# More seven-product pairs in five gate parts, and their last additions moved from VectorE to ScalarE copies and adding DMA

## The chip, the cores and the metric

The kernel runs on one core of a Trainium2 chip, in float32. The metric is the device time of one execution in microseconds. TensorE's clock is granted at its upper level of 2.4 GHz throughout (mean 0.998 of it in the profiled execution).

## The reference, cut to what matters

One layer of a streaming encoder for 256 positions and 2048 channels. The normalised input is projected at once into everything that three attention branches need, and into three gates; the gate projections and the branch projections are where the change lies:

```python
h = _rmsnorm(x, ln_g[l])                                  # 256 x 2048
(qa, ..., zc, ga, gb, gc) = _split_cols(h @ w_in[l])      # ga, gb, gc: 2048 columns each
ya = _mixer_a(...) * jax.nn.silu(za)                      # three attention branches, 256 x 1024 each
yb = _mixer_b(...) * jax.nn.silu(zb)
yc = _mixer_c(...) * jax.nn.silu(zc)
merged = (jax.nn.sigmoid(ga) * (ya @ w_pa[l])
          + jax.nn.sigmoid(gb) * (yb @ w_pb[l])
          + jax.nn.sigmoid(gc) * (yc @ w_pc[l]))
x = x + merged @ w_o[l]
return _rmsnorm(x, final_g)
```

## The kernel before, in words

**Products.** Every float32 matrix product is made of three matmuls of rounded operands: high x high, high x low, low x high. The high part of a weight piece (`w_hi`) is a rounded copy made by ScalarE (L612), the low part (`w_lo`) is the difference made by VectorE (L854). The weights come from HBM in pieces of 128 x 1024 (512 KB) into the slots of `raw`, six of them (`RAWS`); w_hi and w_lo live in a ring of six pieces (`RING`), so ScalarE may write the w_hi of piece n only when TensorE is through with piece n-6. In the stage that matters here both engines prepare a piece four pieces ahead (`FAR`). SyncE loads the slots in order of the pieces, each as soon as VectorE is through with what lay in it: for the first two pieces of a seven-product pair that is after the pair's second sum (waits at L511 and L513).

**Chunks.** The work is a fixed list of chunks, each cut into pieces; each engine runs through the same list with a program of its own. After the attention stage come three branches (b = 0, 1, 2), each as G, P, P, G, P, P. A G chunk ("gate part") computes 1024 columns of one gate projection over all 2048 rows of the weight; a P chunk computes 512 columns of the branch projection, four pieces of four products each. Then come the output chunks, one of which is made like a gate part. The gate part G(b, 0) is called (b, 0) below, the other one (b, 1).

**Pairs.** A gate part's 2048 rows are 16 blocks of 128, taken as eight pairs. For a plain pair ("hh" in the order string of `group_pieces`) TensorE makes eight block products of 128 x 128 x 512, from two pieces of four products. For a seven-product pair ("S") it makes seven, as in the method of Strassen and Winograd: a full piece with two products ("11 22"), a half piece with one ("21 12"), and two pieces of two products that aren't loaded but are sums of the first two, made by VectorE in `usum` ("U1 U3", "U2 U4"). The sums are `sum_13` (L1046, called the first sum here) and `sum_24` (L1056, L1058, the second sum); VectorE issues them at six and five pieces ahead of the piece "U1 U3". All gate parts but the first, (0, 0), have five seven-product pairs and three plain ones, 59 products; (0, 0) has four and four.

**End of a gate part.** The products lie in all eight banks of PSUM. Before the last piece ScalarE copies two banks (`copy_sums`, L718 and L719), VectorE makes four additions with two further banks (`combine`, L1098 to L1105, called the combine), and when TensorE is through, two large additions of the last four banks (`finish_sums`, L1113, called the finish). ScalarE then takes the tanh (L725) at the first two pieces of the following P chunk. A P chunk's result is multiplied by the gate by VectorE (`merge_chunk`, the merge), at the end of the first P chunk and at the first piece of the gate part after the second. For some P chunks of b = 1 and 2 the addition into `merged` is made by an adding DMA that GpSimd issues (L596); the finish writes into the same tile `gx` that holds the gates.

**Who waits.** TensorE waits at the start of a chunk (`banks_free`) until the banks are read out: for a gate part, until the first P chunk before it is merged; for the P chunk behind a gate part, until `copy_sums` is done; for the next one, until the finish is done.

Of the kernel before, what the change touches and what calls it, by code (L numbers as in the profile page):

```python
# [10 lines left out]
ACT = mybir.ActivationFunctionType  # L11

P = 128
# [17 lines left out]

NS = 5
NS_OUT = 3
# [7 lines left out]
def group_pieces(b, u):  # L41

    order = "hhShhShhShhhh" if b == 3 else FIRST_ORDER if (b, u) == (0, 0) else "hShShShShSh"
    n = order.count("S")
    pieces, summed, plain = [], 0, 0
    for k in order:
        if k == "S":
            pieces += [(part, summed) for part in ("11 22", "21 12", "U1 U3", "U2 U4")]
            summed += 1
        else:  # L50
            pieces.append((("p 11 22", "p 21 12")[plain % 2], n + plain // 2))
            plain += 1
    return pieces
# [32 lines left out]
RAW_OF = {g: d for d, g in enumerate(LOADED)}  # L86
ADDED_BY_DMA = [(1, 0), (1, 1), (1, 2), (1, 3), (2, 0), (2, 1)]
COPIED = ("kvc", "v", "uv")
SUMMED = ("q", "k", "uk", "ka")
# [7 lines left out]
RING = 6  # L97
RAWS = 6
WARM = 8
# [99 lines left out]
def hybrid_trunk(nc, x, x_t, w_s, bias, ckv_g, sink, final_g, out):  # L199
# [3 lines left out]
    with ExitStack() as ctx:  # L203
# [45 lines left out]
        with ExitStack() as attention:  # L249
            def early_sb(name, shape):  # L250
                return attention.enter_context(nc.sbuf_tensor(name, shape, F32))

            k_b = early_sb("k_b", [P, 8, SEQ])
            v_b = early_sb("v_b", [P, NT, BW])
            kT_a = early_sb("kT_a", [P, 2, SEQ])
            v_a = early_sb("v_a", [P, NT, 2 * HD])
            v_mid = early_sb("v_mid", [P, 2 * HD])
            work = early_sb("work", [P, SROW])
            causal = early_sb("causal", [P, SROW])
            chosen = early_sb("chosen", [P, SROW])  # L260
            scores = early_sb("scores", [P, 4, SROW])
            probsT = early_sb("probsT", [P, 4, SROW])
            bias_t = early_sb("bias_t", [P, 2, 2, SROW])
            silu = early_sb("silu", [P, 2, SEQ])
# [79 lines left out]
        p_mul = sem("p_mul")  # L344
        merged_added = sem("merged_added")

        zeroed = sem("zeroed")
# [85 lines left out]
        def half_of_sums(k, again):  # L433

            return slice(2, NS_OUT if again else NS) if k else slice(0, 2)

# [123 lines left out]
        def _(pool):  # L560
# [23 lines left out]
            for p in range(NPAIR):  # L584
                if 8 <= p < 16:
# [5 lines left out]
                    pool.wait_ge(bm_ready, 32 * (p - 7))  # L591
            for k, (b, n) in enumerate(ADDED_BY_DMA):
                c = AT["P", b, n]
                pool.wait_ge(dve_evac, dves_before(c + 1))
                wait(pool, merged_added, 16 * k)
                pool.dma_start(merged_v[:, :, CH * n:CH * (n + 1)], gate_of(c), accum_op=ALU.add  # L596
                               ).then_inc(merged_added, 16)
            for t in range(NT):
# [6 lines left out]
        def _(sc):  # L605
# [106 lines left out]
            def copy_sums(c):  # L712
# [6 lines left out]
                nc.scalar.copy(sums[1], bank[3][:, :]).then_inc(g_copied, 1)  # L719

            def tanh_sums(c, parts):

                for a in parts:
                    sc.wait_ge(g_final, NT * sums_of(c) + a // 2 + 1)
                    nc.scalar.activation(gx[:, a, :], gx[:, a, :], ACT.Tanh, scale=0.5).then_inc(tanh_ready, 1)  # L725
# [20 lines left out]
            for c, (kind, b, u) in enumerate(CHUNKS):  # L746
                for j in range(PIECES[c]):
# [50 lines left out]
                    if kind == "G" and j == LAST_SUM[c] + 1:  # L798
                        copy_sums(c)
                    if kind == "P" and KINDS[c - 1] == "G" and j < 2:  # L800
                        tanh_sums(c - 1, (2 * j, 2 * j + 1))
                    if (kind, b, u) == ("P", 2, 3) and j >= 1:
                        transpose_hi(2 * j - 2)
# [11 lines left out]
                    if c == LAST_O and j in (3, 6):  # L815
                        t = j // 6
                        sc.wait_ge(sum_ready, 2 * t + 4)
                        nc.scalar.activation(merged_v[:, t, middle], out_rows[t][:, middle], ACT.Square,
                                              accum_out=ssq_o[:, t, 1:2]).then_inc(sq_ready, 1)
                if kind in ("v", "uv"):  # L820
                    copy_chunk(c)
# [25 lines left out]
        def _(ve):  # L847
# [189 lines left out]
            def sum_13(g):  # L1037
# [3 lines left out]
                wait_source(ve, g - 1)  # L1041
                if SUMS.index(g) == 0:
                    ve.wait_ge(pT_ready, 2 * NPAIR)
                elif SUMS.index(g) == 1:
                    ve.wait_ge(pv_ready, NPAIR // 2)
# [127 lines left out]
            for c, (kind, b, u) in enumerate(CHUNKS):  # L1173
                for j in range(PIECES[c]):
# [108 lines left out]
                    if g in YT_AT:  # L1283
                        yT_split(*YT_AT[g])
                    if kind == "G" and j == 0 and KINDS[c - 1] == "P":
                        merge_chunk(c - 1)
                    if kind == "G" and j == LAST_SUM[c] + 1:
                        combine(c, 0)
                    if kind == "G" and j == min(LAST_SUM[c] + 2, PIECES[c] - 1):
                        combine(c, 1)  # L1290
                    if g + FAR + 2 in SUMS:
                        sum_13(g + FAR + 2)
                    if g + FAR + 1 in SUMS:
                        sum_24(g + FAR + 1)
                    if g == GATES + 1:
# [23 lines left out]
                if kind == "z":  # L1319
                    silu_chunk(c)  # L1320
                if kind == "G" and b < 3:
                    finish_sums(c)
                if kind == "P" and KINDS[c + 1] != "G":
                    merge_chunk(c)
# [39 lines left out]
        def _(pe):  # L1364
# [9 lines left out]
            def banks_free(c):  # L1374
# [17 lines left out]
                if kind == "G":  # L1392
                    pe.wait_ge(g_final, NT * sums_of(c))

# [386 lines left out]
```

## Time and profile before

| | |
|---|---|
| three runs | 943.28, 943.40 and 943.66 us, median 943.4 |
| profiled execution | 943.88 us, its span 941.8 |
| busy: TensorE | 932.6 us, 99% |
| busy: VectorE | 761.8 us, 81% |
| busy: ScalarE | 536.1 us, 57% |
| DMA, mean | 209 GB/s |

A row of time shows the start, the length, the engine, the line and the tiles (out<-in); idle time before it and what ended it stand in brackets. Matmuls are pipelined: each row is longer than the step from one start to the next, so steps are read from the starts. The same holds for VectorE and ScalarE, whose rows overlap the next one by about 0.1 us.

### The profile page before, as it was taken

Reading aid. Unit: us, or ns where it says so; the run is one execution under the profiler, and the core shown is the slowest. Engines: PE = TensorE matmul, PEld = TensorE weight load, DVE = VectorE, ACT = ScalarE, POOL = GpSimd, SP = SyncE. Lnnn points to the kernel's source line nnn. Section 1 sums busy time; section 2 is a strip of 40 time slices with the busy share of each in tenths; the row PEclk is TensorE's granted clock in tenths of the full one; section 3 lists DMA queues with packets and bytes.
Section 4 is the critical chain, followed back from the end, with each engine's and each line's share of the span. In section 5 each row is a group of like instructions: output and inputs, shape, how many; then the busy total and the mean of one; then the engine's idle time right before and its main releaser. Section 6 shows DMA issues by size and latency. Waiting matters only on the chain.

```text
span 941.8 us, 13769 instructions
## 1 busy us (share of the span) xinstructions
PE 932.6 (99%) x5066; PEld 793.2 (84%) x5066; DVE 761.8 (81%) x1306; ACT 536.1 (57%) x916; POOL 32.5 (3%) x40
## 2 busy tenths in 40 slices
PE   9999999999999999999999999999999999999996
PEld 8888888888888888888888888888888888888885
DVE  6585765777756777889998899899997988988993
ACT  6573544466535565667755556465564664654552
POOL 0020000000011110000000000000001000000000
PEclk9999999999999999999999999999999999999999
DMA  8964743666567775556556557467667597664552
GB/s 329 339 206 140 250 157 124 214 231 230 181 183 224 224 224 191 190 191 212 180 180 244 179 187 247 164 208 231 216 223 224 201 373 207 244 224 135 179 179 89
DMA packets 58706, 196.67 MB, mean 209 GB/s; under 512 B 6544, under 2 KB 9488, under 8 KB 58000
## 3 DMA queue, kind: packets, MB, share of 16 engines
q1 hardware_dynamic: 54128, 188.71, 57.9%
q0 software_dynamic: 3936, 6.29, 3.8%
q8 instruction: 40, 0.66, 0.3%
q10 hardware_dynamic: 576, 0.79, 0.2%
q14 instruction: 26, 0.21, 0.1%
HBM read 187.38 MB, written 2.10 MB: 201 GB/s over the span
## 4 chain that ended last, share of the span: by engine, by line
PE 94%; DMA 2%; DVE 1%; issue 1%; SPq 0%; ACT 0%; POOLq 0%; POOL 0%; DVEq 0%
PE bank L1431 24%; PE bank L1441 13%; PE bank L1482 10%; PE bank L1483 10%; PE bank L1481 10%; PE bank L1406 7%; PE bank L1407 7%; PE bank L1408 7%; DMA raw<-in_w_s_dram 2%; PE bank L1368 2%; PE bank L1542 1%; PE bank L1572 1%; DVE w_lo L854 1%; PE bank L1565 0%; PE bank L1690 0%
## 5 line engine op out<-in xcount | busy, mean ns | idle before, releaser
L854 DVE TENSOR_TENSOR w_lo<-raw,w_hi 128x1024 fp32r<-128x1024 f32 (+2 forms) x328 | 369.2, 1154 | 48.0 <-ACT w_hi L612 46.9
L612 ACT ACTIVATE w_hi<-raw 128x1024 fp32r<-128x1024 f32 (+2 forms) x328 | 318.6, 1003 | 71.5 <-PE bank L1408 29.3
L1431 PE MATMUL bank<-hT,w_hi 128*128 128x512 f32 x976 | 236.4, 392 | 0.0
L1431 PEld LDWEIGHTS bank<-hT,w_hi 128*128 128x128 f32 x976 | 178.4, 188 | 34.4
L1441 PE MATMUL bank<-hT,w_lo 128*128 128x256 f32 x976 | 132.1, 284 | 0.0
L1441 PEld LDWEIGHTS bank<-hT,w_lo 128*128 128x128 f32 x976 | 126.4, 191 | 6.6 <-issue 0.9
L612 ACT ACTIVATE w_hi<-usum 128x1024 fp32r<-128x1024 f32 x64 | 68.1, 1064 | 94.9 <-DVE usum L1046 55.9
L1481 PE MATMUL bank<-w_hi,hT 128*128 128x512 f32 x288 | 112.0, 389 | 0.0
L1482 PE MATMUL bank<-w_lo,hT 128*128 128x512 f32 x288 | 112.0, 389 | 0.0
L1483 PE MATMUL bank<-w_hi,hT 128*128 128x512 f32 x288 | 112.0, 389 | 0.0
L854 DVE TENSOR_TENSOR w_lo<-usum,w_hi 128x1024 fp32r<-128x1024 f32 x64 | 78.1, 1222 | 6.7 <-ACT w_hi L612 6.6
L1406 PE MATMUL bank<-w_hi,ybuf 128*128 128x512 f32 x200 | 78.3, 391 | 0.1
L665 ACT ACTIVATE gate<-bank 128x256 f32<-128x256 f32 x69 | 22.7, 383 | 97.0 <-PE bank L1431 88.6
L1407 PE MATMUL bank<-w_lo,ybuf 128*128 128x512 f32 x200 | 77.8, 389 | 0.0
L1481 PEld LDWEIGHTS bank<-w_hi,hT 128*128 128x128 f32 x288 | 54.1, 188 | 11.3
L1482 PEld LDWEIGHTS bank<-w_lo,hT 128*128 128x128 f32 x288 | 54.1, 188 | 11.2
L1483 PEld LDWEIGHTS bank<-w_hi,hT 128*128 128x128 f32 x288 | 54.1, 188 | 11.2
L1408 PE MATMUL bank<-w_hi,ybuf 128*128 128x512 f32 x136 | 52.9, 389 | 0.0
L1408 PE MATMUL bank<-w_hi,hT 128*128 128x512 f32 x128 | 49.8, 389 | 0.0
L1481 PE MATMUL bank<-w_hi,s_hi 128*128 128x512 f32 x128 | 49.8, 389 | 0.0
L1482 PE MATMUL bank<-w_lo,s_hi 128*128 128x512 f32 x128 | 49.8, 389 | 0.0
L1483 PE MATMUL bank<-w_hi,s_lo 128*128 128x512 f32 x128 | 49.8, 389 | 0.0
(212 smaller groups left out, 1116.6 us busy)
## 6 DMA issues: line engine op xcount, KB each, us to landing
raw<-in_w_s_dram SPq DMA_DIRECT2D x314, 512.0 KB, 4.5
bias_t<-in_bias_dram SPq DMA_DIRECT2D x24, 384.0 KB, 3.2
bias_t<-chosen POOLq DMA_DIRECT2D x16, 192.0 KB, 6.8
merged<-big POOLq DMA_DIRECT2D x6, 512.0 KB, 7.2
raw<-in_w_s_dram SPq DMA_DIRECT2D x6, 456.0 KB, 7.6
merged<-in_x_dram SPq DMA_DIRECT2D x2, 1024.0 KB, 14.5
raw<-in_w_s_dram SPq DMA_DIRECT2D x8, 256.0 KB, 3.3
big<-in_x_dram SPq DMA_DIRECT2D x1, 2048.0 KB, 10.1
```

Of the source, the lines that this page charges most:

```text
L612: nc.scalar.activation(halves(g)[0], source(g), ACT.Copy).then_inc(hi_ready, 1)
L665: nc.scalar.activation(gate[:, n % 2, SEQ:CH] if KINDS[c] != "iq" else gate[:, n // 2, SEQ * (n % 2):SEQ * (n % 2 + 1)], bank[base(c) + n] ...
L854: nc.vector.tensor_tensor(low, source(g), high.bitcast(F32), ALU.subtract).then_inc(lo_ready, 1)
L1368: return nc.tensor.transpose(dst, src, ident[0:n, 0:n])
L1406: mm(acc, xh, wh[:, e, :], start=kt == 0, stop=False)
L1407: mm(acc, xh, wl[:, e, :], start=False, stop=False)
L1408: ins = mm(acc, xl, wh[:, e, :], start=False, stop=kt == n_kt - 1)
L1431: ins = mm(bank[base(c) + n][:, :], wh[:, e, n * P:(n + 1) * P], hl_t[:, n_kt * j + e, :, :], start=j == 0 and e == 0, stop=last and e == ...
L1441: ins = mm(bank[base(c) + n][:, 0:SEQ], wl[:, e, n * P:(n + 1) * P], hl_t[:, n_kt * j + e, 0, :], start=False, stop=last and e == n_kt - 1)
L1481: mm(acc, left[0], wh, start=start, stop=False)
L1482: mm(acc, left[0], wl, start=False, stop=False)
L1483: return mm(acc, left[1], wh, start=False, stop=stop)
```

## The change

Five gate parts, all but (0, 0), have six seven-product pairs and two plain ones, 58 products, in the order h SS h SS h SS h. To find room for the larger sums of h, `raw` has five slots instead of six. The finish of every gate part but the last, (2, 1), is made in another way: ScalarE copies the last four banks into the half of `usum` that is free (`copy_rest`), and GpSimd issues two DMAs of 512 KB each that add them to `gx`. The tanh moves to the second and third piece of the second P chunk, the merge of the first P chunk to the fourth piece of the second. The second seven-product pair of each changed part has its sums issued three pieces sooner. The first sum of all waits for the last attention product (`pv_ready`) instead of the last transposes (`pT_ready`).

```diff
-NS = 5
+NS = 6
 NS_OUT = 3
...
-    order = "hhShhShhShhhh" if b == 3 else FIRST_ORDER if (b, u) == (0, 0) else "hShShShShSh"
+    order = "hhShhShhShhhh" if b == 3 else FIRST_ORDER if (b, u) == (0, 0) else "hSShSShSSh"
     n = order.count("S")
...
 ADDED_BY_DMA = [(1, 0), (1, 1), (1, 2), (1, 3), (2, 0), (2, 1)]
+LAST_GROUP = AT["G", 2, 1]
+LAST_U = {c: max(g for g in SUMS if PART[g][0] == c) for c in USES}
+SOON = [3 if PART[g][0] != AT["G", 0, 0] and sum(PART[k][0] == PART[g][0] for k in SUMS[:n]) == 1 else 0
+        for n, g in enumerate(SUMS)]
 COPIED = ("kvc", "v", "uv")
...
 RING = 6
-RAWS = 6
+RAWS = 5
 WARM = 8
...
         merged_added = sem("merged_added")
+        rest_copied = sem("rest_copied")
+        rest_added = sem("rest_added")
...
-            return slice(2, NS_OUT if again else NS) if k else slice(0, 2)
+            m = NS_OUT if again else NS
+            return slice((m + 1) // 2, m) if k else slice(0, (m + 1) // 2)
+
+        def finish_parts(c):
+
+            return usum[:, SUMS.index(LAST_U[c]) % 2, :, :]
...
                     pool.wait_ge(bm_ready, 32 * (p - 7))
-            for k, (b, n) in enumerate(ADDED_BY_DMA):
-                c = AT["P", b, n]
-                pool.wait_ge(dve_evac, dves_before(c + 1))
-                wait(pool, merged_added, 16 * k)
-                pool.dma_start(merged_v[:, :, CH * n:CH * (n + 1)], gate_of(c), accum_op=ALU.add
-                               ).then_inc(merged_added, 16)
+            for c, (kind, b, n) in enumerate(CHUNKS):
+                if kind == "G" and c < LAST_GROUP:
+                    pool.wait_ge(g_comb, 4 * sums_of(c) + 4)
+                    for t in range(NT):
+                        pool.wait_ge(rest_copied, NT * sums_of(c) + t + 1)
+                        pool.dma_start(gx[:, 2 * t:2 * t + 2, :].rearrange("p n s -> p (n s)"),
+                                       finish_parts(c)[:, t, :], accum_op=ALU.add).then_inc(rest_added, 16)
+                if kind == "P" and (b, n) in ADDED_BY_DMA:
+                    pool.wait_ge(dve_evac, dves_before(c + 1))
+                    wait(pool, merged_added, 16 * ADDED_BY_DMA.index((b, n)))
+                    pool.dma_start(merged_v[:, :, CH * n:CH * (n + 1)], gate_of(c), accum_op=ALU.add
+                                   ).then_inc(merged_added, 16)
             for t in range(NT):
...
+            def copy_rest(c):
+
+                sc.wait_ge(used, FIRST[c + 1])
+                for t in range(NT):
+                    nc.scalar.activation(finish_parts(c)[:, t, :].rearrange("p (n s) -> p n s", n=2),
+                                         pair[2 + t][:, :, :], ACT.Copy).then_inc(rest_copied, 1)
+
             def tanh_sums(c, parts):
+                if c < LAST_GROUP:
+                    sc.wait_ge(rest_added, 32 * sums_of(c) + 32)
                 for a in parts:
-                    sc.wait_ge(g_final, NT * sums_of(c) + a // 2 + 1)
+                    if c == LAST_GROUP:
+                        sc.wait_ge(g_final, a // 2 + 1)
                     nc.scalar.activation(gx[:, a, :], gx[:, a, :], ACT.Tanh, scale=0.5).then_inc(tanh_ready, 1)
...
                         copy_sums(c)
-                    if kind == "P" and KINDS[c - 1] == "G" and j < 2:
+                    if kind == "P" and c - 1 == LAST_GROUP and j < 2:
                         tanh_sums(c - 1, (2 * j, 2 * j + 1))
+                    if kind == "P" and KINDS[c - 2] == "G" and c - 2 < LAST_GROUP and j in (1, 2):
+                        tanh_sums(c - 2, (j - 1, j + 1))
                     if (kind, b, u) == ("P", 2, 3) and j >= 1:
...
                                               accum_out=ssq_o[:, t, 1:2]).then_inc(sq_ready, 1)
+                if kind == "G" and c < LAST_GROUP:
+                    copy_rest(c)
                 if kind in ("v", "uv"):
...
                 wait_source(ve, g - 1)
-                if SUMS.index(g) == 0:
-                    ve.wait_ge(pT_ready, 2 * NPAIR)
-                elif SUMS.index(g) == 1:
+                if SUMS.index(g) < 2:
                     ve.wait_ge(pv_ready, NPAIR // 2)
...
                         yT_split(*YT_AT[g])
+                    if kind == "P" and KINDS[c - 2] == "G" and c - 2 < LAST_GROUP and j == 3:
+                        merge_chunk(c - 1)
                     if kind == "G" and j == 0 and KINDS[c - 1] == "P":
...
                         combine(c, 1)
-                    if g + FAR + 2 in SUMS:
-                        sum_13(g + FAR + 2)
-                    if g + FAR + 1 in SUMS:
-                        sum_24(g + FAR + 1)
+                    for n, k in enumerate(SUMS):
+                        if k - FAR - 2 - SOON[n] == g:
+                            sum_13(k)
+                        if k - FAR - 1 - SOON[n] == g:
+                            sum_24(k)
                     if g == GATES + 1:
...
                     silu_chunk(c)
-                if kind == "G" and b < 3:
+                if c == LAST_GROUP:
                     finish_sums(c)
-                if kind == "P" and KINDS[c + 1] != "G":
+                if kind == "P" and KINDS[c + 1] != "G" and c > LAST_GROUP:
                     merge_chunk(c)
...
                 if kind == "G":
-                    pe.wait_ge(g_final, NT * sums_of(c))
+                    pe.wait_ge(g_comb, 4 * sums_of(c))
+                    if c - 2 == LAST_GROUP:
+                        pe.wait_ge(g_final, NT)
+                    else:
+                        pe.wait_ge(rest_copied, NT * sums_of(c))
```

## Rows read from the trace of the kernel before

**Rows 1.** Page, the chain that ended last: share of the span by engine.

```profile
PE 94%; DMA 2%; DVE 1%; issue 1%; SPq 0%; ACT 0%; POOLq 0%; POOL 0%; DVEq 0%
```

**Rows 2.** Waits of TensorE, all of them: total us, times, longest us.

```profile
PE bank L1596 <- DVE hT L1159: 1.4, 1, 1.4
```

**Rows 3.** Busy time by stages: one period (G, P, P), us busy of each engine.

```profile
578.00:640.00 62.00, 62.00 (x275) 51.33 (x274) 56.26 (x58) 35.78 (x40) 0.00 (x0) 1.00 0.60 204
```

**Rows 4.** Timeline of TensorE: first matmul of gate part (1, 0), and first behind it.

```profile
597.85 0.39 PE L1481 MATMUL bank<-w_hi,hT 128*128 128x512 f32 x1
...
637.97 0.39 PE L1406 MATMUL bank<-w_hi,y_odd_hi 128*128 128x512 f32 x1
```

**Rows 5.** Timeline of VectorE around and in gate part (1, 0).

```profile
593.76 1.23 DVE L854 TENSOR_TENSOR w_lo<-usum,w_hi 128x1024 fp32r<-128x1024 f32 x1
...
598.05 1.22 DVE L1028 SCALAR_TENSOR_TENSOR merged<-big,bank 128x1024 f32<-128x1024 f32 x1 [0.34 <-PE bank L1408]
...
601.92 1.23 DVE L854 TENSOR_TENSOR w_lo<-raw,w_hi 128x1024 fp32r<-128x1024 f32 x1 [1.50 <-ACT w_hi L612]
603.06 1.22 DVE L1046 TENSOR_TENSOR usum<-raw 128x1024 f32<-128x1024 f32 x1
604.20 0.68 DVE L854 TENSOR_TENSOR w_lo<-raw,w_hi 128x512 fp32r<-128x512 f32 x1
604.80 0.69 DVE L1056 TENSOR_TENSOR usum<-usum,raw 128x512 f32<-128x512 f32 x1
605.52 0.69 DVE L1058 TENSOR_TENSOR usum<-usum,raw 128x512 f32<-128x512 f32 x1
606.13 2.44 DVE L854 TENSOR_TENSOR w_lo<-usum,w_hi 128x1024 fp32r<-128x1024 f32 x2
608.49 2.35 DVE L854 TENSOR_TENSOR w_lo<-raw,w_hi 128x1024 fp32r<-128x1024 f32 x2
...
631.57 5.76 DVE L854 TENSOR_TENSOR w_lo<-raw,w_hi 128x1024 fp32r<-128x1024 f32 x5
637.24 0.68 DVE L1098 TENSOR_TENSOR big<-big,bank 128x512 f32<-128x512 f32 x1
...
640.07 2.35 DVE L1113 TENSOR_TENSOR big<-big,bank 128x1024 f32<-128x1024 f32 x2
```

**Rows 6.** Timeline of ScalarE in the same part: a w_hi, and the two bank copies.

```profile
600.83 1.06 ACT L612 ACTIVATE w_hi<-raw 128x1024 fp32r<-128x1024 f32 x1 [1.66 <-PE bank L1483]
...
635.45 0.59 ACT L718 COPY big<-bank 128x512 f32<-128x512 f32 x1 [0.23 <-PE bank L1483]
635.93 0.59 ACT L719 COPY big<-bank 128x512 f32<-128x512 f32 x1
```

**Rows 7.** DMA: loads (L514, 670 to 690), adding DMAs (L596), their queue (651 to 660).

```profile
DMA to landing us min/median/max: 3.4/3.5/4.6
...
DMA to landing us min/median/max: 6.9/7.2/8.8
...
q0 software_dynamic: 272, 0.52, 31.9%
```

**Rows 8.** Around the end of part (2, 0): issue of x, a stage (last but one: DMA share), a w_hi.

```profile
753.98 0.42 SPq L545 DMA_DIRECT2D big<-in_x_dram  x1
...
768.00:772.00 4.00, 4.00 (x20) 3.30 (x19) 2.27 (x2) 4.00 (x6) 0.00 (x0) 1.00 1.03 414
...
772.97 1.06 ACT L612 ACTIVATE w_hi<-raw 128x1024 fp32r<-128x1024 f32 x1 [0.15 <-DMA raw<-in_w_s_dram]
```

**Rows 9.** Startup: a load in the chain (issue to landing), and TensorE's wait behind it.

```profile
18.86 15.31 DMA raw<-in_w_s_dram
...
36.57 0.19 PEld L1406 LDWEIGHTS bank<-w_hi,ybuf 128*128 128x128 f32 x1 [0.55 <-DVE w_lo L854]
```

**Rows 10.** Last attention products on TensorE, and VectorE's first sum of all.

```profile
469.06 1.53 PE L1542 MATMUL bank<-probsT,rows 128*64 128x128 f32 x24
...
468.20 1.22 DVE L1046 TENSOR_TENSOR usum<-raw 128x1024 f32<-128x1024 f32 x1
```

More of the change, by code:

```diff
@@ L260, in hybrid_trunk @@
             chosen = early_sb("chosen", [P, SROW])
+            early_sb("s_end", [P, P])
             scores = early_sb("scores", [P, 4, SROW])
```

## The prediction

> **What bounds the kernel now.** The chain of waits comes first: 94% of the span is TensorE [rows 1]. The waits of TensorE name one, 1.4 us at the start [rows 2]; in the gate stage it never waits. The view by stages shows how near the next engine is: of 62 us (one period: a gate part and two P chunks) VectorE is busy 56.3, ScalarE 35.8 [rows 3]. So TensorE is the bound, VectorE 5.7 us behind it, and where those 5.7 us lie decides this case. TensorE's timeline gives the unit: gate part (1,0) starts at 597.85 and the P chunk behind it at 637.97, 59 products of three matmuls in 40.12 us, 0.680 us per product u [rows 4]; a P chunk of 16 products is 10.9 us. VectorE's timeline [rows 5] shows an idle 1.50 us before 601.92 and then one unbroken run from 603.06 to 637.2, through the whole gate part. Its steps, start to start (us): w_lo of a full piece 1.14 (601.92 to 603.06; two usum pieces from 606.13 to 608.49, 1.18 each), of a half piece 0.60; the first sum of a pair 1.14, the second 0.72 + 0.61 = 1.33; a merge 1.15; a finish 2.27 for both halves. A seven-product pair costs it 1.14 + 1.14 + 0.60 + 1.33 + 2.36 = 6.56, while TensorE spends 7u = 4.76 on it. A plain pair, two pieces, costs 2.27 against 8u = 5.44 on TensorE. Seven-product pairs are lost ground for VectorE and plain pieces win it back: 7.69 against 11u = 7.48 for one pair and one plain piece.
>
> **What TensorE saves.** Five gate parts have 58 products instead of 59: 5 x 0.680 = 3.4 us. If nothing else moved: 940.0.
>
> **Load of VectorE.** Per changed part +6.56 - 2.27 for the pair and -2.27 for the finish: +2.0 in a period of 61.5, so 58.3 busy. On the average it still fits. It must be followed in order, since the ring of six pieces forbids it to run ahead: w_hi of piece n waits until TensorE has begun piece n-5, 0.26 later (piece 6 of the part shown at 600.83, TensorE's piece 1 at 597.85 + 4u), and w_lo follows 1.09 behind, at 601.92 [rows 5, 6].
>
> Time 0 is TensorE's start of the gate part. Its order is h SS h SS h SS h (pieces 0 to 27); a pair takes 2u, 1u, 2u, 2u, an h 4u. TensorE begins piece 1 at 4u = 2.7, 2 at 6u = 4.1, 16 at 32u = 21.8, 21 at 43u = 29.3, 25 at 50u = 34.0, and ends at 58u = 39.5. VectorE's w_lo of piece 3 starts at -4.1 as before (593.76), then come the merge of the first P chunk to -1.8, the second sum of pair 2 to -0.4 (issued three pieces sooner than the rule for the others has it, its first sum is done by then), w_lo of 4 to 0.7, the merge of the second P chunk to 1.9, w_lo of 5 to 3.0; piece 6 waits for the ring to 3.6, piece 7 to 5.4 (4.08 + 0.26 + 1.09). From there it is unbroken: pieces 7 and 8 2.36; 9 and 10 2.27; rest of pair 3 (both sums, the half piece, two usum pieces) 5.43; piece 14 1.14; rest of pair 4 5.43; 18 and 19 2.27; rest of pair 5 5.43; 23 1.14; first sum, piece 24 and second sum of pair 6 1.14 + 0.60 + 1.33. That is 28.5: piece 25 starts at 33.95 and is written 1.22 later, at 35.2. TensorE wants it at 34.0. Margins at 16 and 21 are 0.9 and 0.7; at 25 it is -1.2. By the same count the order of before has at least 2 us everywhere (its w_lo of piece 25 is through at 632.7, wanted at 635.3). I take **1.17 us per part, 5.8 us** in all; bounds 0.5 and 1.9 per part (a semaphore step more or less at each of some five hand-overs of ScalarE).
>
> **End of the gate part.** Copies and combine stand behind the w_hi and w_lo of the fourth piece of the next chunk. With five raw slots the third and fourth wait for the slots of pair 6, free with its second sum at 33.95. A load lands 3.5 us later [rows 7], the second 1.3 behind: 38.8; w_hi to 39.8; two bank copies of 0.48 + 0.59 [rows 6] to 40.8, and TensorE, which waits for them before the P chunk, is there at 39.5 + 1.2 = 40.6. Before, the same copies began at 635.45, 2.5 early. I take **0.2 per part, 1.0**; from 0 to 1.0 each (loads land up to 4.6 after issue).
>
> **The finish by ScalarE and DMA.** Let E be TensorE's end of the part. The two bank copies (some 1.0 each, twice the 0.48 of a half) are done by E+2.3. VectorE, late now, ends w_lo at E+1.4 and the combine (2.83, 637.24 to 640.07) at E+4.2, and POOL issues only then: E+4.25 and, after 1.2, E+5.45. An adding DMA of this size exists in the trace: 6.9 to 8.8 us to landing, 7.2 typical, and in its 9 us it took 31.9% of the 16 engines, 2.9 us of all of them [rows 7]. Below: both as if alone, the second lands at E+12.7. Above: one behind the other, E+18.7. They share engines with each other and with about four raw loads of 1.3 us issued from E+5.4: I take E+15.0.
> Who waits: tanh in the second P chunk, one piece after E+10.9, at E+12.1. Behind it on ScalarE: w_hi of piece 2, tanh, w_hi of 3; on VectorE w_lo of 2, second sum, first sum of pair 2, w_lo of 3, then the merge, which TensorE needs to begin the next gate part. From landing: 1.1 + 0.6 + 0.6 + 1.3 + 1.1 + 1.2 + 1.2 = 7.1. The next part is due at E+21.8, so the landing may be at E+14.6 for nothing. At 15.0 it costs 0.4: three parts, **1.2**; from 0 to 4 each. Behind part (0,0), unchanged and not late, the DMAs go out 3 us sooner: nothing.
> Part (2,0) ends about 761.5, and x and final_g, 3 MB, were issued at 753.98 and after; the engines are full at 768 to 772 (share 1.03), and a w_hi waited for its load at 772.97 [rows 8]. There 8.8 replaces 7.2 and the loads themselves are late: **2.0**, from 0.5 to 5.
>
> The Trainium skill, "DMA: Bandwidth & Descriptors", section "Anatomy of one DMA", gives a GpSimd-issued DMA 2.0 us plus bytes over 436 GB/s; for 512 KB that is an estimate of 3.2 us. By it the landing would be E+8.7, no part would start late and the sum would be 3.2 us smaller. The rows, 7.2 for an adding one, disagree, and I go by them.
>
> **At nothing.** Five raw slots elsewhere: early loads already queue 15.3 us in the DMA engines, and a later issue does not move their landing; if it did, TensorE, which waited 0.55 there, would lose up to 2 [rows 9]. The first pair's sum now waits for the last attention product, 470.6 instead of 468.20 [rows 10]: w_lo of piece 3 is then at 474.9, wanted no sooner than 470.6 + 7u = 475.4; gone, that cover costs 1. ScalarE's two copies and one and a half more w_hi per part, 3.6 us: it has 26 us idle per period [rows 3]. Tanh and merge in the second P chunk instead of the first: nobody asks for them sooner, as long as the landing is in time.
>
> **Sum.** The profiled execution is 943.88 (span 941.8 and 2.1 around it), 0.5 above the median 943.4. 943.9 - 3.4 + 5.8 + 1.0 + 1.2 + 2.0 = 950.5; against the median **950.0**, 0.7% slower.
>
> **Rivals.**
> 1. Only the stall inside the parts: both adding DMAs land by E+14.6 everywhere and the copies are in time. 943.4 - 3.4 + 5.8 = 945.8. For it: a single one takes 7.2 and 14.6 leaves 9.1. Against it: two at once, with loads.
> 2. The other side, faster: VectorE's lead covers the 50u. It happens if w_lo of piece 25 starts 1.2 us sooner, as it would if pieces 6 and 7 did not wait for the ring (1.8 us idle before 5.4) because the parts start late by themselves, or if VectorE's steps were 4% (1.2 of 28.5) shorter than those of [rows 5]. Then the copies and the DMAs find it in time too, and it is 940.0. Against it: the steps of [rows 5] repeat to a hundredth in all five periods. It decides at 1.2 us per part.
> 3. The DMA engines are the bound around the merges: landings at E+17 in three parts (2.4 each) and 5 in the last, 943.4 - 3.4 + 5.8 + 1.0 + 7.2 + 5 = 959. For it: share 1.03 in [rows 8]. Against it: in the three parts before, the engines have pauses. Halfway to it from the forecast lies 954.5.
> 4. It moves less than counted: stall and saving even out, 943 to 945.
>
> **Chances.** Forecast 0.45, rival 1 0.2, rival 2 0.1, rival 3 0.15, rival 4 0.1. Range 943.0 to 955.5; the forecast's own is 946.5 to 953. Runs of this kernel differ by 0.4 us; 0.2% (1.9 us) is what one can tell. Faster: rival 2 and a little, 0.11. Within: rival 4 and the lower edge of rival 1, 0.15. Slower 0.74.
>
> **What would show it.** TensorE's waits: in each changed part one for w_lo near piece 25, 1.2 us, none in (0,0); w_hi of the P chunk's fourth piece near TensorE's end; a wait of TensorE for a merge at the start of part (2,1), the longest, and small ones before; landing of the adding DMAs at 8 to 10 us from issue. Wrong if TensorE has no waits in the gate stage (then 940), or if the waits sit at the startup or in the attention stage.

## The result, and the profile after

The changed kernel takes 960.0 us (median of 4 runs, 959.78 to 960.82) against 943.5 (943.28 to 943.68): 16.5 us slower, ratio 1.0177 with the interval 1.0159 to 1.0194. The forecast was 950.0, with a range up to 955.5. The direction was right, and the measured time lies 10 us above the forecast. The profiled execution of the new kernel has a span of 959.0, 17.2 over the 941.8 of before.

From the page, the chain that ended last (answers to [rows 1]):

```profile
PE 70%; DVE 18%; DMA 6%; issue 4%; ACT 1%; POOL 0%; SPq 0%; POOLq 0%; DVEq 0%; ACTq 0%
```

The waits of TensorE's matmuls (total us, times, longest; answers to [rows 2], where only the 1.4 stood); three more groups of 0.7, 0.2 and 0.2 us are left out:

```profile
PE bank L1518 <- DVE big L1062: 7.1, 3, 6.6
PE bank L1518 <- DVE w_lo L886: 4.8, 5, 1.0
PE bank L1633 <- DVE hT L1189: 1.4, 1, 1.4
PE bank L1443 <- DVE w_lo L886: 0.7, 1, 0.7
...
```

Where they lie shows in the timeline of TensorE's weight loads; in brackets is the idle time before each, and what ended it. The rows ahead of the dots are one whole pattern, those behind them the place that breaks it. L1518 is a gate part, L1443 a P chunk:

```profile
571.23 0.19 PEld L1518 LDWEIGHTS bank<-w_hi,s_hi 128*128 128x128 f32 x1 [1.38 <-DVE w_lo L886]
576.99 0.19 PEld L1443 LDWEIGHTS bank<-w_hi,ybuf 128*128 128x128 f32 x1 [0.45 <-issue]
599.24 0.19 PEld L1518 LDWEIGHTS bank<-w_hi,hT 128*128 128x128 f32 x1 [0.60 <-DVE merged L1060]
634.51 0.19 PEld L1518 LDWEIGHTS bank<-w_hi,s_hi 128*128 128x128 f32 x1 [1.38 <-DVE w_lo L886]
...
784.43 0.19 PEld L1443 LDWEIGHTS bank<-w_hi,ybuf 128*128 128x128 f32 x1 [1.13 <-DVE w_lo L886]
787.32 0.19 PEld L1443 LDWEIGHTS bank<-w_hi,ybuf 128*128 128x128 f32 x1 [0.26 <-DVE w_lo L886]
796.93 0.29 PEld L1518 LDWEIGHTS bank<-w_hi,hT 128*128 128x128 f32 x1 [7.04 <-DVE big L1062]
```

Each of the five changed parts has its 1.38 inside, then 0.39 to 0.73 before the P chunk behind it, then 0.60 to 0.72 before the next part. Part (0,0) has none. The pattern breaks between (2,0) and (2,1): the P chunk waits inside, and the wait at 796.93, before (2,1), is ten times as long as at the other starts. Behind it comes something that no row of before had. In the stages view (us, busy time and count of TensorE, of its weight loads, VectorE, ScalarE, GpSimd, then granted clock, DMA share, GB/s):

```profile
792.00:796.00 4.00, 0.00 (x0) 0.00 (x0) 3.96 (x6) 2.88 (x3) 0.00 (x0) 0.92 0.33 91
797.00:800.00 3.00, 3.00 (x7) 2.42 (x8) 2.96 (x4) 0.00 (x0) 1.20 (x1) 0.50 0.65 174
800.00:804.00 4.00, 4.00 (x14) 3.15 (x13) 2.31 (x3) 0.79 (x2) 1.19 (x1) 0.72 0.79 169
```

The clock fell while TensorE stood idle (0.92 as the mean of 792 to 796). Then TensorE ran at a granted clock of 0.50, its 1.2 GHz level, for some 5 us. Its own timeline says what that cost: twelve matmuls take 0.43 us from start to start (the first 0.59) instead of 0.23.

```profile
796.94 0.80 PE L1518 MATMUL bank<-w_hi,hT 128*128 128x512 f32 x1 [6.62 <-DVE big L1062]
797.53 0.63 PE L1519 MATMUL bank<-w_lo,hT 128*128 128x512 f32 x1
...
801.80 0.59 PE L1520 MATMUL bank<-w_hi,hT 128*128 128x512 f32 x1
802.22 0.40 PE L1518 MATMUL bank<-w_hi,hT 128*128 128x512 f32 x1
802.45 0.39 PE L1519 MATMUL bank<-w_lo,hT 128*128 128x512 f32 x1
```

The account, in us of span, goes through these rows and the others of the pattern, which are not shown. Inside the parts it is 5 x 1.25 = 6.2: TensorE's starts lie 1.35 apart there instead of 0.23, and the next step is 0.1 wider. That is the 1.38 less 0.13, and 0.13 is taken off each of the others too. The rest: before P chunks 2.1; part starts (1,0), (1,1), (2,0) 1.5; inside P chunk (2,1) 1.1; start of (2,1) 6.9; slow clock 12 x 0.2 = 2.4. The sum is 20.2, less the 3.4 of saved products 16.8, of a measured 17.2.

Why the start of (2,1) is so late stands in the timelines of the other engines. SyncE's has the issue of x and final_g, 3 MB together:

```profile
764.10 0.43 SPq L557 DMA_DIRECT2D big<-in_x_dram  x1
764.57 0.47 SPq L559 DMA_DIRECT2D fin_g<-in_final_g_dram  x1
```

ScalarE's, behind the end of part (2,0):

```profile
767.17 1.94 ACT L743 ACTIVATE usum<-bank 128x1024 f32<-128x1024 f32 x2
769.00 1.06 ACT L630 ACTIVATE w_hi<-raw 128x1024 fp32r<-128x1024 f32 x1
778.30 1.06 ACT L630 ACTIVATE w_hi<-raw 128x1024 fp32r<-128x1024 f32 x1 [8.24 <-DMA raw<-in_w_s_dram]
782.06 1.06 ACT L630 ACTIVATE w_hi<-raw 128x1024 fp32r<-128x1024 f32 x1 [2.70 <-DMA raw<-in_w_s_dram]
784.95 1.06 ACT L630 ACTIVATE w_hi<-raw 128x1024 fp32r<-128x1024 f32 x1 [1.83 <-DMA raw<-in_w_s_dram]
...
788.44 1.14 ACT L753 ACTIVATE big<-big 128x512 f32<-128x512 f32 x2
```

VectorE's, in the same stretch:

```profile
779.39 1.23 DVE L886 TENSOR_TENSOR w_lo<-raw,w_hi 128x1024 fp32r<-128x1024 f32 x1 [7.37 <-ACT w_hi L630]
...
790.33 1.23 DVE L1076 TENSOR_TENSOR usum<-raw 128x1024 f32<-128x1024 f32 x1 [0.54 <-DMA raw<-in_w_s_dram]
...
795.67 1.21 DVE L1062 SCALAR_TENSOR_TENSOR big<-big,bank 128x1024 f32<-128x1024 f32 x1
```

The part ended at about 766.9, so x went out 2.8 before its end; in the kernel before it was 7.5 before the end [rows 8]. The raw load behind the 3 MB came 8.24 us late for ScalarE, the next ones 2.70 and 1.83 late. VectorE waited for the w_hi behind them (7.37, 2.54, 1.66) and once more for a raw load (0.54). From 790.33 it had no pause until the merge at 795.67, and TensorE began behind it. Tanh, at 788.44, waited for no adding DMA (they were issued at 771.2 and 772.0 and took 13.5 at most): it stood behind the same late loads. It was done by 791.9, so the merge did not wait for tanh but for its place in VectorE's order.

### The profile page after: what moved, and what is told of

It is laid out like the page before. It is cut to its first block, busy times and chain, and to the rows that moved or that the text cites. A ratio compares the mean times of both kernels' runs of the same rounds, so it can differ in the third digit from the quotient of the medians.

```text
span 959.0 us, 13824 instructions
## 1 busy us (share of the span) xinstructions
PE 936.1 (98%) x5051; PEld 791.5 (83%) x5051; DVE 772.4 (81%) x1321; ACT 552.3 (58%) x936; POOL 41.3 (4%) x50
## 4 chain that ended last, share of the span: by engine, by line
PE 70%; DVE 18%; DMA 6%; issue 4%; ACT 1%; POOL 0%; SPq 0%; POOLq 0%; DVEq 0%; ACTq 0%
PE bank L1468 24%; PE bank L1478 13%; DVE w_lo L886 11%; PE bank L1443 4%; PE bank L1445 4%; PE bank L1444 4%; PE bank L1518 4%; PE bank L1520 4%; PE bank L1519 4%; DMA big<-usum 3%; DVE usum L1076 3%; DMA raw<-in_w_s_dram 2%; PE bank L1453 2%; PE bank L1401 2%; DVE usum L1086 2%
## 5 line engine op out<-in xcount | busy, mean ns | idle before, releaser
L630 ACT ACTIVATE w_hi<-usum 128x1024 fp32r<-128x1024 f32 x74 | 77.9, 1060 | 86.3 <-DVE usum L1076 55.9
L1518 PE MATMUL bank<-w_hi,hT 128*128 128x512 f32 x263 | 103.9, 395 | 7.5 <-DVE big L1062 7.1
L1519 PE MATMUL bank<-w_lo,hT 128*128 128x512 f32 x263 | 103.3, 393 | 0.0
L1520 PE MATMUL bank<-w_hi,hT 128*128 128x512 f32 x263 | 103.2, 393 | 0.0
L886 DVE TENSOR_TENSOR w_lo<-usum,w_hi 128x1024 fp32r<-128x1024 f32 x74 | 89.7, 1221 | 2.9 <-ACT w_hi L630 2.9
L1443 PE MATMUL bank<-w_hi,ybuf 128*128 128x512 f32 x200 | 78.7, 393 | 1.1 <-DVE w_lo L886 0.7
L1518 PEld LDWEIGHTS bank<-w_hi,hT 128*128 128x128 f32 x263 | 50.0, 190 | 20.0 <-DVE big L1062 8.4
L1518 PE MATMUL bank<-w_hi,s_hi 128*128 128x512 f32 x148 | 58.2, 393 | 4.8 <-DVE w_lo L886 4.8
L1520 PEld LDWEIGHTS bank<-w_hi,hT 128*128 128x128 f32 x263 | 49.9, 190 | 10.6
L1519 PEld LDWEIGHTS bank<-w_lo,hT 128*128 128x128 f32 x263 | 49.9, 190 | 10.3
L1519 PE MATMUL bank<-w_lo,s_hi 128*128 128x512 f32 x148 | 57.6, 389 | 0.0
L1520 PE MATMUL bank<-w_hi,s_lo 128*128 128x512 f32 x148 | 57.6, 389 | 0.0
L1445 PE MATMUL bank<-w_hi,hT 128*128 128x512 f32 x128 | 49.8, 389 | 0.0
```

Of the source, the lines that this page charges most:

```text
L630: nc.scalar.activation(halves(g)[0], source(g), ACT.Copy).then_inc(hi_ready, 1)
L886: nc.vector.tensor_tensor(low, source(g), high.bitcast(F32), ALU.subtract).then_inc(lo_ready, 1)
L1443: mm(acc, xh, wh[:, e, :], start=kt == 0, stop=False)
L1445: ins = mm(acc, xl, wh[:, e, :], start=False, stop=kt == n_kt - 1)
L1518: mm(acc, left[0], wh, start=start, stop=False)
L1519: mm(acc, left[0], wl, start=False, stop=False)
```

## Experiments

**1. x and final_g sooner.** Only their place is changed.

```diff
-                if g == FIRST[AT["P", 2, 1]]:
+                if g == FIRST[AT["G", 2, 0]] + 15:
```

> The changed kernel, with the loads of x and final_g (3 MB) issued 16 pieces after the start of gate part (2,0) instead of with the first piece of P chunk (2,1). In the changed kernel TensorE waits 6.6 us before part (2,1), some 1.4 us in the P chunk before it, and the granted clock is 0.50 for the 3 us behind the wait. Theory (the 3 MB stand in the load queue ahead of the pieces, because with five slots SyncE comes to them later): these waits shrink to the 0.6 us of the other parts and the clock stays at 1.0: 949 to 951. Rival (the two adding DMAs behind part (2,0) hold the engines): x has little to do with it, 957 or more. Rival (the 3 MB do the same harm wherever they stand): the wait shows up inside part (2,0), 957 to 960.

Measured: 951.65 us, ratio 1.0083 (1.0066 to 1.0100), just above the 949 to 951 expected. x was issued at 732.15, the start of (2,1) waits 0.42, the clock is 1.00 there. The five inner waits stayed; the one in (2,0) grew to 1.92, and a smaller one of 0.38 stands before it, in the part that the 3 MB now go beside.

```profile
762.52 0.19 PEld L1518 LDWEIGHTS bank<-w_hi,s_hi 128*128 128x128 f32 x1 [1.92 <-DVE w_lo L886]
790.41 0.19 PEld L1518 LDWEIGHTS bank<-w_hi,hT 128*128 128x128 f32 x1 [0.42 <-DVE big L1062]
```

So 8.4 of the 16.5 us hang on the place of these 3 MB.

**2. VectorE makes the finish.** The adding DMAs and ScalarE's copies behind the gate parts go; tanh and merge stay late, x stays in its place. Of the edit only the place in VectorE's program is shown.

```diff
-                if c == LAST_GROUP:
-                    finish_sums(c)
+                if kind == "G" and b < 3:
+                    finish_sums(c)
...
```

> The changed kernel with the finish made by VectorE as before in all six gate parts, no adding DMAs behind them, tanh and merge still in the second P chunk. Theory (order of the loads is the cause at part (2,1), the adding DMAs only add to it): the waits of 0.6 us at the starts of (1,0), (1,1), (2,0) go, at (2,1) 5.8 us of engine time are gone from the queue but x still stands ahead: 951 to 955, with the five waits of about 1 us for w_lo inside the parts unchanged. Rival (the adding DMAs are the cause of everything outside the parts): 947 to 949. Rival (VectorE has no room for the finish): it falls behind in the P chunks, 960 or more.

Measured: 950.44 us, 1.0071 (1.0056 to 1.0086): 9.6 us less than the changed kernel and a little below the 951 to 955 expected, though x is issued at 763.12, again some 3 us before the end of the part. Start of (2,1):

```profile
789.19 0.19 PEld L1504 LDWEIGHTS bank<-w_hi,hT 128*128 128x128 f32 x1 [1.36 <-DVE big L1051]
```

The small waits at the other part starts are gone, the inner 1.38 and those before P chunks are all there. ScalarE's timeline shows, by comparison, what the adding DMAs had done:

```profile
775.23 1.06 ACT L624 ACTIVATE w_hi<-raw 128x1024 fp32r<-128x1024 f32 x1 [7.67 <-DMA raw<-in_w_s_dram]
776.52 1.06 ACT L624 ACTIVATE w_hi<-raw 128x1024 fp32r<-128x1024 f32 x1 [0.23 <-DMA raw<-in_w_s_dram]
...
780.35 1.06 ACT L624 ACTIVATE w_hi<-raw 128x1024 fp32r<-128x1024 f32 x1 [0.21 <-DMA raw<-in_w_s_dram]
781.32 1.14 ACT L744 ACTIVATE big<-big 128x512 f32<-128x512 f32 x2
```

The 3 MB cost one long wait here too, 7.67. But the loads behind it then follow at once, and tanh comes at 781.32 instead of 788.44. From issue to landing of the raw loads issued from 766 to 790 (min, median, max), in the changed kernel, in experiment 2 and in experiment 1:

```profile
DMA to landing us min/median/max: 5.4/12.5/17.9
```

```profile
DMA to landing us min/median/max: 3.7/5.1/11.8
```

```profile
DMA to landing us min/median/max: 3.5/6.1/9.6
```

The kernel before, without adding DMAs there and with x at its earlier time, has 4.5, 5.3 and 7.1 in this window. So either burden alone hardly moves the median, though the 3 MB raise the longest one to 11.8; both together make the median 12.5.

**3. Five raw slots alone**, in the kernel before.

```diff
-RAWS = 6
+RAWS = 5
```

> The kernel before with five raw slots instead of six, nothing else. Theory (in the old order a slot comes free early enough nearly everywhere; x and final_g come a piece later and do some harm at part (2,1)): 943.5 to 945.5, no wait of TensorE elsewhere. Rival (the fifth slot costs loads at the startup and in the attention stage): 946 or more, with new waits before 470 us. Rival (the jam behind (2,0) is made by five slots alone): a wait of several us at the start of (2,1), 948 to 953.

Measured: 943.41 us, 0.9999 (0.9990 to 1.0008), as expected but for the small harm at (2,1), which did not come. No wait of TensorE is new. x was issued at 756.54, 2.6 later than in [rows 8].

**4. The new finish alone**: order of before, 59 products, six slots; only ScalarE's copies, the adding DMAs, and tanh and merge later.

```diff
-NS = 6
+NS = 5
...
-    order = "hhShhShhShhhh" if b == 3 else FIRST_ORDER if (b, u) == (0, 0) else "hSShSShSSh"
+    order = "hhShhShhShhhh" if b == 3 else FIRST_ORDER if (b, u) == (0, 0) else "hShShShShSh"
...
-RAWS = 5
+RAWS = 6
...
```

> The kernel before (six slots, order h S h S h S h S h S h, 59 products) with only the finish by ScalarE copies and adding DMAs and the later tanh and merge. Theory (VectorE is not late at the end of a part here, so the adding DMAs are issued some 3 us sooner and land in time; x stands sooner too): 943 to 945, no waits of TensorE in the gate stage or small ones before (2,1). Rival (the adding DMAs hold up the loads by themselves): 947 to 952, with waits at part (2,1).

Measured: 947.58 us, 1.0037 (1.0024 to 1.0050). The expectation, 943 to 945, was missed, and its rival (the adding DMAs hold up the loads by themselves) came true. In the profiled execution one wait of TensorE is new, and it is at the same place, although x went out at 753.71, as early as before:

```profile
786.03 0.19 PEld L1519 LDWEIGHTS bank<-w_hi,hT 128*128 128x128 f32 x1 [3.07 <-DVE big L1061]
```

The five executions spread from 946.15 to 948.89 us. The profiled one, 946.37, is one of the two short ones, with a mean granted clock of 0.999; the three long ones have 0.995 and 0.996, and the changed kernel has 0.994 and 0.995. That points to a longer wait with the slow clock behind it in those three, but no trace of them shows it.

Experiments 2 to 4 and the changed kernel make a square for the start of (2,1), though not a clean one: experiment 2 has the changed order of pairs, 4 has not. With neither burden (experiment 3, and before) there is no wait. With the adding DMAs and x at its old time it is 3.07 (and with x out of the way, in experiment 1, 0.42). With x late and no adding DMAs it is 1.36. With both it is 7.04, and the slow clock, 2.4, comes on top. The two together cost about 9.4, their single waits 4.4. By the median of experiment 4, 3.8 above the kernel before, the single ones come to some 5, which is still little more than half.

**5. The first sum of the third pair sooner**, on top of experiment 1. The ring leaves VectorE 0.3 to 0.9 us idle early in a changed part; a sum that needs no ring place can fill it. `third` is true for the third pair of each changed part; its definition is left out.

```diff
-                        if k - FAR - 2 - SOON[n] == g:
+                        if k - FAR - 2 - (4 if third else SOON[n]) == g:
```

> As e1_x_sooner (x and final_g issued in gate part (2,0)), and the first sum of the third seven-product pair of each changed part issued four pieces sooner, into VectorE's idle time while pieces 6 and 7 wait for the ring. Theory (the wait for w_lo of piece 25 is VectorE's count: it starts its unbroken run too late by the time that the ring keeps it idle): the 1.14 us of that sum leave the run, piece 25 is late by 0.1 instead of 1.2, about 1.2 us less per part: 951.7 - 5 to 6 = 945.5 to 947. Rival (the wait is set by the raw slots or by ScalarE's w_hi, not by VectorE's own count): no change, 951 to 952. Rival (the margins at pieces 16 and 21 are the next to be late): half of it, 948 to 950.

Measured: 950.39 us, 1.0072 (1.0058 to 1.0085). The expectation, under 947, was missed. VectorE's timeline early in parts (0,1) and (1,0):

```profile
540.52 1.22 DVE L1076 TENSOR_TENSOR usum<-raw 128x1024 f32<-128x1024 f32 x1
541.65 2.35 DVE L886 TENSOR_TENSOR w_lo<-usum,w_hi 128x1024 fp32r<-128x1024 f32 x2
...
602.93 1.22 DVE L1076 TENSOR_TENSOR usum<-raw 128x1024 f32<-128x1024 f32 x1
604.07 2.35 DVE L886 TENSOR_TENSOR w_lo<-usum,w_hi 128x1024 fp32r<-128x1024 f32 x2
```

The idle time is gone, and the inner wait went from 1.38 to 0.47 in (0,1), and to 0.98 to 1.02 in three of the others. Part (2,0), with the 3 MB, kept its 1.91 and got more: 0.50 and 0.85 before it, where experiment 1 has one of 0.38. A sum of 1.14 us can only save the idle time that it fills. Before the same w_lo experiment 1 has 0.71 of it in (0,1) and 0.29 in (1,0); the waits shrank by 0.9 and 0.4. VectorE is then without a pause from the P chunk into the part.

**6. Copies and combine ahead of the last piece's w_hi and w_lo**, on top of experiment 1.

```diff
+                    first = kind == "G" and b < 3 and j == LAST_SUM[c] + 1
+                    if first:
+                        copy_sums(c)
                     for later in ahead(g):
                         hi(later)
...
+                    if first:
+                        combine(c, 0)
+                        combine(c, 1)
                     for later in ahead(g):
                         lo(later)
...
```

> As e1_x_sooner, and at the last piece of a gate part the two bank copies of ScalarE stand ahead of the w_hi of the fourth piece of the next chunk, and VectorE's combine ahead of its w_lo. Theory: the waits of 0.4 to 0.7 us at the start of each P chunk behind a changed part go (the w_hi in front of the copies waited for its raw slot), and the adding DMAs are issued 1.1 us sooner, so the waits of 0.4 to 0.6 at the start of the parts go too; the waits for w_lo of piece 25 stay: 951.7 - 2.2 - 1.8 = 947.5 to 948.5. Rival (the starts of the parts are held by the engines' load, not by the issue): 949 to 950. Rival (VectorE, blocked until the copies are done, is late in the P chunk): 951 or more.

Measured: 954.76 us, 1.0120 (1.0105 to 1.0136), 3.1 slower than experiment 1, where 947.5 to 948.5 were expected. The waits before P chunks are gone, as meant, but every part start is later; (1,0):

```profile
600.38 0.19 PEld L1525 LDWEIGHTS bank<-w_hi,hT 128*128 128x128 f32 x1 [1.64 <-DVE merged L1063]
```

Its ScalarE has the reason. The adding DMAs go out 1.4 sooner (580.30 for 581.70), the w_hi that was overtaken starts 0.6 later (576.21), and the raw loads then meet the DMAs:

```profile
584.08 1.06 ACT L630 ACTIVATE w_hi<-raw 128x1024 fp32r<-128x1024 f32 x1 [1.54 <-DMA raw<-in_w_s_dram]
589.01 1.06 ACT L630 ACTIVATE w_hi<-raw 128x1024 fp32r<-128x1024 f32 x1 [3.87 <-DMA raw<-in_w_s_dram]
```

The merge came 0.6 later than in experiment 1, and TensorE was there 0.5 sooner: 1.64 for 0.55. Which of the two shifts makes the load late was not separated.

**7. Both, 5 and 6.**

> The changed kernel with all three: x sooner, the third pair's first sum sooner, copies and combine ahead. Theory (saving 3.4, and each of the three waits taken away on its own): 943.6 - 3.4 + 0.5 to 1.5 for what is left = 940.7 to 941.7, faster than the kernel before. Rival (a new wait takes the place of those, as the adding DMAs beside x do in e4_offload_alone): 943 to 946.

Measured: 953.25 us, 1.0103 (1.0090 to 1.0117). Missed as 6 was, by 12 us: the inner waits are about 1.0 (1.92 in (2,0)), those at the part starts 0.83 to 1.88.

**8. The same with the finish by VectorE** (the edits of 1, 2, 5 and 6).

> As e6_all, but with the finish made by VectorE in all parts and no adding DMAs behind them. Theory (VectorE has 5.7 us idle per period in the P chunks, the finish of 2.3 fits there): same as e6_all or up to 0.5 us faster, 940.2 to 941.5. Rival (with six seven-product pairs VectorE needs the offload): waits of TensorE at the start of the parts or inside, 943 or more.

Measured: 944.55 us, 1.0012 (1.0003 to 1.0020). It was expected at 940.2 to 941.5, so this too was missed, but it is 8.7 less than 7, from which only the finish differs. The inner waits are 0.24 in three parts, 0.99 in (1,1), 1.89 in (2,0), where the 3 MB pass.

**9. As 8, x and final_g at their old place.**

> The kernel after with VectorE finishing all sums (no adding DMAs behind the gate parts), the third pair's first addition four pieces sooner, bank copies and additions ahead of the last piece's w_hi and w_lo; x and final_g at their place of before and after (piece 0 of P chunk (2,1)). Same as the last experiment but for x. Theory (3 MB beside a changed gate part costs VectorE's lead there; beside the P chunk it is harmless only if no adding DMA follows): the 1.89 us wait inside (2,0) falls to 0.24-1.0, and a wait at the start of (2,1) of 0.5-1.4 us comes in its place: 943.5-945. Rival (x at its old place was the whole of the loss, with or without adding DMAs): a wait of over 3 us at the start of (2,1) and 947 or more.

Measured: 945.07 us, 1.0018 (1.0009 to 1.0027). The wait in (2,0) fell to 0.25, the start of (2,1) waits 1.67, a little over the 0.5 to 1.4 expected, and the inner one of (2,1) is 0.97. The rival (over 3 us) is out.

With it there is a clean pair on either side: only the place of the 3 MB differs between the changed kernel and experiment 1, and between 9 and 8. With adding DMAs behind the parts the late place costs 8.4 us (960.0 for 951.65), without them 0.5 (945.07 for 944.55). The harm is in the meeting of the two.

**10. As 8, x at piece 15 of (2,0), final_g at piece 15 of (2,1).**

```diff
+                if g == FIRST[AT["G", 2, 0]] + 15:
                     sp.wait_ge(yT_lo, 6)
                     sp.dma_start(x_res, x_v).then_inc(res_in, 16)
+                if g == FIRST[AT["G", 2, 1]] + 15:
                     sp.wait_ge(used, END["P", 1, 3])
```

> As the last one, but x (2 MB) is loaded at piece 15 of part (2,0) and final_g (1 MB to all partitions) at piece 15 of part (2,1). Theory (a part has room for about 1 MB to 2 MB more beside its weights before the raw loads come late for VectorE): the wait inside (2,0) falls from 1.89 to about 1.0, the one in (2,1) grows from 0.24 to 0.5-1.0: 943.5-944.5. Rival (the whole of the 1.89 us is VectorE's own queue in that part, as 0.99 us is in (1,1) where nothing but weights is loaded): (2,0) stays at 1.0-1.9 and (2,1) stays 0.24: 944-944.6. To beat the kernel before it would have to be under 943.3.

Measured: 942.55 us, 0.9990 (0.9981 to 0.9999): 0.9 us below the kernel before, and the interval just excludes no gain. Theory (943.5 to 944.5) and rival (944 to 944.6) were both missed. The loads beside (2,0) and (2,1) no longer cost anything: the inner waits there are 0.24 and 0.25. The one of (1,1) is still 1.03. Of its TensorE waits, the longest groups:

```profile
PE bank L1628 <- DVE hT L1182: 1.4, 1, 1.4
PE bank L1513 <- DVE w_lo L879: 0.6, 1, 0.6
...
```

## Why the prediction was right or wrong

**Saved products, 3.4: right.** Experiment 10 shows it where hardly anything waits. Its parts (0,1) and (1,0) begin here:

```profile
536.08 0.39 PE L1513 MATMUL bank<-w_hi,hT 128*128 128x512 f32 x1
...
597.41 0.39 PE L1513 MATMUL bank<-w_hi,hT 128*128 128x512 f32 x1
```

That is 61.33 for the period, against 61.88 in the kernel before (535.97 to 597.85), with an inner wait of 0.25 left in it (0.12 by the count above): 0.67 saved, forecast 0.680.

**Inner stall, 5.8 forecast, 6.2 found: right**, in size and place: one wait for w_lo in each of the five parts, at the piece forecast, and none in (0,0). It comes with and without the new finish (experiments 1 and 2) and never with the old order (3 and 4). VectorE's unbroken run is the cause: experiment 5 shifts it by the idle time it fills and the wait shrinks by about as much. The prediction counted 1.8 us of idle time ahead of that run; 0.28 to 0.31 were there in three parts and 0.91 in (0,1), since the merges come later than counted. That did not change the stall, but it is the main reason why experiment 5 gained 1.3 us and not 5. Rival 2, that VectorE's lead covers the part, is refuted.

**Bank copies, 1.0 forecast, 2.1 found.** The order is the reason, as forecast: experiment 6 takes these waits away by it alone. With 0.39 to 0.73 they lie inside the bound of 1.0 each. But the prediction let the w_hi in front wait for raw slots and their loads. ScalarE's timeline at the end of (0,1) shows another wait:

```profile
570.08 1.06 ACT L630 ACTIVATE w_hi<-usum 128x1024 fp32r<-128x1024 f32 x1 [0.86 <-DVE usum L1088]
571.04 4.93 ACT L630 ACTIVATE w_hi<-raw 128x1024 fp32r<-128x1024 f32 x5
575.87 0.57 ACT L736 COPY big<-bank 128x512 f32<-128x512 f32 x1
```

It waits for VectorE's second sum of pair 6 and then writes six w_hi nearly without a pause. The only wait for a load that its rows show in this place is one of 0.20, in (2,1). No run has the changed order with six slots, so what the fifth slot adds here is open, but the trace leaves it little.

**Finish by ScalarE and DMA at three part starts, 1.2 forecast, 1.5 found: right.** Experiment 2 removes these waits. The six DMAs behind (0,1), (1,0) and (1,1) landed 6.7 to 10.7 after their issue. Tanh waited for them (1.74, 1.95 and 2.48) until 15.4 to 15.6 us after the end of the part, where 15.0 was forecast and 14.6 would have cost nothing, and TensorE began 7.2 after tanh did, where 7.1 was forecast. The margin was thin: VectorE waits for a raw load in the same stretch, and without tanh in the way it would have been only 0.2 us sooner.

**Part (2,0) to (2,1), 2.0 forecast (0.5 to 5), about 10.4 found (1.1 + 6.9 + 2.4): this is the step that failed**, and 8.4 of the 10 us that were missing. It read "8.8 replaces 7.2 and the loads themselves are late" and took x as issued at 753.98, as before. Three things were wrong in it.
- The issue moved. SyncE's queue issues x when it comes to the place in its order, and what stands ahead waits for raw slots. x went out 2.8 before the part's end instead of 7.5. Five slots alone move it by 2.6 (experiment 3).
- The term was mainly for the adding DMA's landing. What was late were raw loads that were in flight together with it and stood behind the 3 MB: 8.24, 2.70 and 1.83 on ScalarE, against 7.67 and 0.23 without the adding DMAs. Tanh, VectorE's w_lo and the merge are all queued behind them. The clean pairs say the same: the late place costs 8.4 with the adding DMAs and 0.5 without. The share of 1.03 in [rows 8] had shown the engines full there; rival 3 took it up, with 5 us, and was the nearest of the rivals in total (959). Its 2.4 at each of the three other starts did not come.
- The clock. A wait of 6.6 was followed by a stretch at 0.50, another 2.4, for which the sum had no term.

**At nothing.** Five slots elsewhere: right for the old order (experiment 3, 0.9999), and no wait is new at the startup with the new one. First sum, ScalarE's load, later tanh and merge: no wait stands at them outside those named.

## What to carry over

Where the DMA engines are full in one stage of the trace (DMA share 1.03), price added transfers there by what stands behind them on every engine that waits for a load, and ask anew when the big one is issued: a transfer in an ordered queue moves with everything ahead of it. Two burdens on the same engines need not simply add: waits of 3.1 and 1.4 alone became 7.0 together. A wait of TensorE as long as that one has to be counted with the slow clock behind it. An engine whose average load fits can still hold up the one that bounds the kernel where its work is bunched; follow its order step by step, which was right here to 7%.

## What was not expected of the hardware

- After 6.6 us without a matmul TensorE ran at a granted clock of 0.50 (1.2 GHz) and took twelve matmuls at 0.43 us before 0.23 came back. After the longest wait of experiment 4 in its profiled execution (its matmul timeline has 2.65) and behind the inner waits of the changed kernel (0.96 us and the like), the granted clock stayed at 1.00; experiment 4, 786 to 789:

```profile
786.00:789.00 3.00, 2.97 (x13) 2.44 (x14) 3.00 (x3) 0.00 (x0) 1.20 (x1) 1.00 0.96 307
```

- 512 KB DMAs that add, issued in pairs, took 4.7 to 13.5 us to land (median 10.0), against 6.9 to 8.8 one by one in the kernel before [rows 7]; beside the 3 MB, behind (2,0), 10.5 and 13.5.
